# Output projection of a decoder layer: one full-precision product against three products of hi and lo parts

## The chip, the cores and the metric

The kernel runs on one core of one Trainium2 chip. Its time is the device time of one execution in microseconds; the median of the runs is compared. One execution was also taken by the hardware profiler, and all rows below come from that one.

## What is computed

Two layers of a decoder trunk for 512 prompt tokens and 32 sample tokens (T = 544 columns), 1,024 features (8 blocks of 128). Each layer runs a half FFN, a mixer with three branches (chunked gating, forgetting attention, mLSTM), and a second half FFN. The change lies at the end of the mixer:

```python
def merge_branches(ys, gates, w_branch, w_out):
    m = gates[:, :, 0] * (ys[0] @ w_branch[0])
    for nb in range(1, N_BRANCH):
        m = m + gates[:, :, nb] * (ys[nb] @ w_branch[nb])
    return m @ w_out

x = x + mod[:, 1, 2][:, None] * merge_branches((ya, yb, yc), gates, w_branch, w_out)
x = half_ffn(x, mod[:, 2], g_norm[2], w_ff_up[1], w_ff_down[1])
```

## The kernel before

Features lie on the partitions, tokens along the columns; a matmul works on half of the tokens (272 columns). All engines run programs written out by hand, and semaphores order them.

**Two ways to multiply.** Most products (both FFNs, the input projections, the gates) are made of parts. ScalarE copies a block of weights, 128x1024, into a tile of type fp32r ("hi"), and VectorE subtracts that from the raw block, in place, which gives the rest ("lo"). The activations are split in the same way (`HH` and `HX` for the mixer's input). TensorE then adds three fp32r products per pair of blocks: hi by hi, lo of the activations by hi, hi of the activations by lo (`thirds`, L934). The three branch products and the output projection multiply raw fp32 by raw fp32 instead, one `mm` for each pair of blocks; the trace shows such an `mm` as two matmul records.

**Who splits the mixer's weights.** `JOBS` lists the splits in order; `hi_part` (ScalarE, L1416) and `lo_part` (VectorE, L1754) must be called in that order, and `piece` (L437) says where a block's raw weights, hi and lo lie. TensorE waits in `split_in` for the lo.

**The merge.** For each branch (order a, c, b) and each of 8 feature blocks m there are four steps of TensorE: two gate halves (24 fp32r products each) and two branch halves (4 fp32 products each), each half in its own PSUM bank. ScalarE reads a gate half through Tanh (L1451) and then makes the hi of the next block's gate weights. VectorE reads a branch half: (gate + 1) times product (L2066), added to the merged sum `MT` (L2070). With branch b, the last one, the addition raises `s_m`; after its two halves, block m of `MT` is final. This last branch is `LAST_MERGE`.

**The output projection.** TensorE waits for all 16 halves:

```python
pe.wait_ge(s_m, 2 * KD * (l + 1))
apart(pe)
for i in range(OUT_STEPS):
    s = weights(l, f"out{i}")
    w = W[s][:, :].rearrange("p (k n) -> p k n", k=KD)
    for b in range(4):
        product(unit(), [w[:, k, b * P:(b + 1) * P] for k in range(KD)], lambda k: MT[:, k, :])
```

That is 8 output blocks ("units"), each 8 input blocks by 2 halves, 128 `mm` in a layer. Two pairs of PSUM banks take turns, so unit i+2 waits until unit i is read. VectorE reads a unit with the gate into `X` (`add_block`, L1840, called by `add_to_x`), ScalarE squares that block of `X` for the next norm (`squares`, L1344), and the next FFN begins when all 8 squares are summed.

**Weights.** SyncE's queue loads weight steps of 2 MB into two slots in turn, each when the step before in that slot is released. `out0` takes the slot of the last but one merge step, `out1` that of the last; ahead of `out1` the same queue brings `X` back, whose place the lo activations `HX` had held until the last gate.

Of the kernel before, what the change touches and what calls it, by code (L numbers as in the profile page):

```python
# [19 lines left out]
ACT = mybir.ActivationFunctionType  # L20
ALU = mybir.AluOpType
AX = mybir.AxisListType

P = 128
L = 2
D = 1024
KD = D // P
# [3 lines left out]
T = NP + NS  # L31
HALF = T // 2
# [148 lines left out]
JOBS += [(name, i) for name in ("qkc", "vc", "oc") for i in range(4)]  # L181
JOBS += [("qk", i) for i in range(8)] + [("vb", i) for i in range(4)]
JOBS += [("merge", i) for i in range(3 * KD)]
JOB = {job: i for i, job in enumerate(JOBS)}
LAST_GATE = max(u for u, (what, _, _) in enumerate(FILLS) if what.startswith("gate"))

# [87 lines left out]
def build(nc, d, out):  # L274
    ctx = ExitStack()
    with ctx:
# [9 lines left out]
        def sem(name):  # L286
            return ctx.enter_context(nc.semaphore(name))
# [39 lines left out]
        def over(name, start, *shape, dt=F32R):  # L327
            return sb(name, [P] + list(shape), dt, over=area_at + 4 * start)
# [12 lines left out]
        def take(*shape, start=None):  # L341
# [7 lines left out]
            if len(shape) > 1:  # L349
# [67 lines left out]
                        vc=[over(f"w_hi_vc{i}", o_g + 4096 + 1024 * i, 1024) for i in range(4)],  # L417
                        vb=[over(f"w_hi_vb{i}", o, 1024) for i, o in enumerate((o_k + 1280, o_g, o_g + 1024))]
                        + [WHM[0]])
        WFH = over("wfi_hi", o_r - T, KD, 44)  # L420

        G = ctx.enter_context(nc.psum_tensor("g", [P, 4, 512], F32))
# [14 lines left out]
        def piece(l, job):  # L437

            kind, i = job
            if kind == "rows":  # L440
                return None, WFI[:, :, :], WFH[:, :, :], WFL[:, :, :]
            if kind == "qk":
                name, o, hi = ("qb", "kb")[i // 4], None, WHM[i % 2]
            elif kind == "merge":
                name, o, hi = f"{'acb'[i // KD]}{i % KD // 2}", i % 2 * UP_BLOCK, WHM[(i + 1) % 2]
            else:
                name, o = kind, None
                hi = VALUE_HI[kind][i] if kind in VALUE_HI else (LATER_HI if kind == "oc" else FIRST_HI)[i]
            hi = hi[:, :]
            s = slot_of(l, name)  # L450
            if o is not None or kind in VALUE_HI:
                o = i * 1024 if o is None else o
                return name, W[s][:, o:o + 1024], hi, WR[s][:, o:o + 1024]
            cols = slice(i % 4 * P, (i % 4 + 1) * P)
            return (name, W[s][:, :].rearrange("p (k n) -> p k n", k=KD)[:, :, cols],
                    hi.rearrange("p (k n) -> p k n", k=KD), WR[s][:, :].rearrange("p (k n) -> p k n", k=KD)[:, :, cols])
# [91 lines left out]
        s_fd = sem("half_unit_read_by_dve")  # L548
        s_xs = sem("x_stored")
        s_xr = [sem("x_loaded0"), sem("x_loaded1")]  # L550
        s_mh = sem("mixer_weights_hi")
        s_ml = sem("mixer_weights_split")
        s_ks = sem("sample_fox_keys_done")
# [29 lines left out]
        def apart(eng):  # L583

            eng.sem_inc(s_apart, 1)
# [192 lines left out]
        def _(pe):  # L778
# [22 lines left out]
            def unit():  # L801

                p = un.k % 2
                pe.wait_ge(s_dr[p], un.d[p].value())
                un.take()
                return p
# [3 lines left out]
            def weights(l, i):  # L810

                at = AT["mix", (l, i)]
                if asked[0] != at:
                    pe.wait_ge(s_w[at % 2], LANDED[at])
                    asked[0] = at
                return at % 2
# [26 lines left out]
            def product(p, blocks, rhs, m=P, first=None):  # L843

                n = len(blocks)
                for k in range(n):
                    if first is not None:
                        wait(first)
                    for h in range(2):
                        last = mm(G[0:m, 2 * p + h, 0:HALF], blocks[k], rhs(k)[:, h * HALF:(h + 1) * HALF],  # L850
                                  k == 0, k == n - 1)
                last.then_inc(s_unit, 1)
# [78 lines left out]
                while turned:  # L931
                    features(turned.pop())

            def thirds(o, hi, lo, k, h, begin, end):  # L934

                cols = slice(h * HALF, (h + 1) * HALF)
                for i, (w, x) in enumerate(((hi, HH), (hi, HX), (lo, HH))):
                    last = mm(o, w, x[:, k, cols], begin and i == 0, end and i == 2)
                return last

# [71 lines left out]
            for l in range(L):  # L1012
# [279 lines left out]
                turn_back(1)  # L1292
                pe.wait_ge(s_ybs, 2 * (l + 1))
                fill(l, LAST_MERGE, 1)
                pe.wait_ge(s_m, 2 * KD * (l + 1))
                apart(pe)
                for i in range(OUT_STEPS):
                    s = weights(l, f"out{i}")
                    w = W[s][:, :].rearrange("p (k n) -> p k n", k=KD)
                    for b in range(4):  # L1300
                        product(unit(), [w[:, k, b * P:(b + 1) * P] for k in range(KD)], lambda k: MT[:, k, :])
                norm_sums(ada_before(l, 1))
                norm_roots(3 * l + 2, ada_before(l, 1))
                ffn(l, 1)
# [3 lines left out]
        def _(ac):  # L1308
# [32 lines left out]
                outs.n += 1  # L1341
                ac.dma_start(dst, src).then_inc(s_outa, 16)

            def squares():  # L1344
                for k in range(KD):
                    wait(t["xup"])
                    ac.activation(H[:, k, :], X[:, k, :], ACT.Square).then_inc(s_sq, 1)

            def roots(n):

# [10 lines left out]
            def ffn(l, f):  # L1361

                plan, at, ada = ffn_plan(), [0], ada_after(l, f)

                def split():

                    i = at[0]
                    at[0] += 1
                    step, o, n = plan[i]
                    place = AT["ffn", (l, f, step)] % 2  # L1370
                    if i == 0 or plan[i - 1][0] != step:
                        ac.wait_ge(s_w[place], LANDED[AT["ffn", (l, f, step)]])
                    ac.activation(WH[i % 2][:, 0:n], W[place][:, o:o + n], ACT.Copy).then_inc(s_wh, 1)  # L1373

                def after(i):
                    if ada[i] is not None:
                        rows(ADA_ORDER.index(ada[i]))

                def first_splits():
                    ac.wait_ge(s_unit, un.u.value())  # L1380
                    split()
                    split()

                def chunk(c):
                    p = mine()
                    split()
                    drained(ac.activation(halves(SIL[:, c % 2, :]), both(p), ACT.Silu, bias=ZERO[:, 0:1]), p)  # L1387
                    mine()
                    split()

                if l or f:
                    squares()
                first_splits()
                if l or f:
                    roots(3 * l + 2 * f)
                for k in range(KD):
                    wait(t["tn"])
                    ac.activation(HH[:, k, :], TN[:, k % 2, :], ACT.Copy).then_inc(s_hh, 1)
                i = 0
                for blocks in FF_PART:  # L1400
                    for c in range(blocks):
                        chunk(c)
                        if c % 2 == 1:
                            after(i)
                            i += 1
                    for m in range(KD):
                        mine()
                        if at[0] < len(plan):
                            split()
                        if m % 2 == 1:  # L1410
                            after(i)
                            i += 1
# [55 lines left out]
            for l in range(L):  # L1468
# [204 lines left out]
                read(l, IN_SAMPLE.early[-1])  # L1673

                ac.wait_ge(s_outa, outs.value())
                for tick in range(3):
                    read(l, LAST_MERGE.early[tick] + LAST_MERGE.late[tick])
                un.take(KD)
                ffn(l, 1)
            ac.wait_ge(s_outa, outs.value())  # L1680
# [3 lines left out]
        def _(ve):  # L1684
# [69 lines left out]
            def lo_part(l, *jobs):  # L1754

                for job in jobs:
                    assert split[0] == len(JOBS) * l + JOB[job], (job, JOBS[split[0] % len(JOBS)])
                    split[0] += 1
                    _, raw, hi, lo = piece(l, job)
                    ve.wait_ge(s_mh, split[0])  # L1760
                    ve.tensor_tensor(lo, raw, hi, ALU.subtract).then_inc(s_ml, 1)
# [95 lines left out]
                    link(last)  # L1857

            def add_to_x(gate, l):
                for i in range(KD // 2):  # L1860
                    for j in range(2):
                        p = mine()
                        if i % 2 == 0 and j == 0:
                            ve.wait_ge(s_xr[i // 2], 16 * (l + 1))
                        add_block(X[:, bass.ds(i * 2 + j, 1), :].rearrange("p a n -> p (a n)"),
                                  MOD[:, bass.ds(i * 2 + (gate + j), 1), :].rearrange("p a n -> p (a n)"), p, j, True)

            ve.memset(EPSC[:, 0:1], EPS)
            ve.memset(EPSC[:, 1:2], DB * EPS)
# [17 lines left out]
            for l in range(L):  # L1887
# [287 lines left out]
                masked(1)  # L2175
                read(IN_SAMPLE.early[-1])
                own(1)
                for tick in range(3):
                    read(LAST_MERGE.early[tick] + LAST_MERGE.late[tick])
                ve.sem_inc(s_smallf, 1)  # L2180
                add_to_x(24 + 16, l)
                ffn(l, 1)
# [101 lines left out]
```

## Time and profile before

| what | value |
| --- | --- |
| median of 3 runs | 3396.11 us (3390.53 to 3396.54) |
| the profiled execution | 3397.05 us, span 3395.4 us |
| mean granted TensorE clock | 0.958 of 2.4 GHz |
| TensorE busy | 3168.6 us (93%) |
| VectorE busy | 1197.4 us (35%) |
| ScalarE busy | 821.1 us (24%) |
| output projection, each layer | 58.92 us |

Busy time is the union of an engine's instructions; matmuls overlap, so the mean of one (0.29 us) is longer than the time from one to the next. The granted clock is a share of 2.4 GHz.

### The profile page before, as it was taken

The numbers are of one execution on the slowest core, as the hardware profiler recorded it, in microseconds if no ns is written. First come the engines' busy times: TensorE is split into PE (matmuls) and PEld (weight loads), VectorE is DVE, ScalarE is ACT, GpSimd is POOL, SyncE is SP. The second block draws the span as 40 slices with busy tenths as digits, with TensorE's granted clock in tenths as the row PEclk, the third lists the DMA queues.
The fourth block names the chain that finished last, engine by engine and source line by source line (L and its number), as shares of the span: only waits on it lengthen the run. The fifth ranks groups of instructions, "written<-read, shape, count | busy, mean of one in ns | idle before, by whom it ended". The sixth has DMA issues, their size and how long they took to land.

```text
span 3395.4 us, 53600 instructions
## 1 busy us (share of the span) xinstructions
PE 3168.6 (93%) x23198; PEld 2818.9 (83%) x23198; DVE 1197.4 (35%) x2031; ACT 821.1 (24%) x1202; POOL 138.4 (4%) x269
## 2 busy tenths in 40 slices
PE   5999999989799998999989999899888999989999
PEld 4999988758676787999979999787676768889998
DVE  3332334234532214333343333431444322153333
ACT  2211224223431112212222122232234311122121
POOL 0000000000302000000000000000012110000000
PEclk9999999989899999999989999898888999999999
DMA  5444431202138432232313433321021473212221
GB/s 230 149 156 168 149 139 51 88 25 72 60 113 270 149 116 75 100 149 100 112 75 137 161 137 143 132 76 63 27 71 60 159 259 118 108 71 88 93 82 73
DMA packets 117723, 390.76 MB, mean 115 GB/s; under 512 B 12672, under 2 KB 63200, under 8 KB 99184
## 3 DMA queue, kind: packets, MB, share of 16 engines
q1 hardware_dynamic: 99456, 338.36, 27.8%
q0 software_dynamic: 14432, 34.09, 2.9%
q10 hardware_dynamic: 3600, 14.89, 1.1%
q8 instruction: 183, 3.00, 0.4%
q14 instruction: 52, 0.43, 0.0%
HBM read 373.61 MB, written 13.69 MB: 114 GB/s over the span
## 4 chain that ended last, share of the span: by engine, by line
PE 80%; DVE 9%; DMA 5%; ACT 3%; SPq 1%; issue 1%; ACTq 0%; DVEq 0%
PE g L796 72%; PE q L796 4%; PE tb L796 4%; DMA w<-in_w_up 2%; DVE area L2086 1%; DMA area<-in_w_ada 1%; DVE area L1736 1%; DMA area<-in_cache_v 1%; DVE area L1737 1%; DVE w_lo L1795 1%; DVE area L1990 1%; ACT w_hi L1373 1%; DVE h_lo L1748 1%; SPq L660 1%; DMA area<-in_cache_k 0%
## 5 line engine op out<-in xcount | busy, mean ns | idle before, releaser
L796 PE MATMUL g<-h_hi,w_hi 128*128 128x272 f32 x2816 | 593.3, 292 | 37.5 <-DVE h_lo L1748 24.2
L796 PE MATMUL g<-h_hi,w_lo 128*128 128x272 f32 x2816 | 586.8, 290 | 0.0
L796 PE MATMUL g<-h_lo,w_hi 128*128 128x272 f32 x2816 | 583.8, 288 | 0.0
L1373 ACT ACTIVATE w_hi<-w 128x1024 fp32r<-128x1024 f32 (+2 forms) x240 | 274.2, 1144 | 1260.3 <-PE g L796 932.6
L1795 DVE TENSOR_TENSOR w_lo<-w,w_hi 128x1024 fp32r<-128x1024 f32 (+2 forms) x240 | 319.3, 1332 | 509.2 <-ACT w_hi L1373 505.9
L796 PEld LDWEIGHTS g<-h_hi,w_hi 128*128 128x128 f32 x2816 | 446.3, 191 | 59.3 <-ACT area L1387 28.2
L796 PEld LDWEIGHTS g<-h_lo,w_hi 128*128 128x128 f32 x2816 | 445.3, 190 | 0.0
L796 PEld LDWEIGHTS g<-h_hi,w_lo 128*128 128x128 f32 x2816 | 444.4, 190 | 0.0
L796 PE MATMUL g<-h_hi,w_rest 128*128 128x272 f32 x1152 | 341.4, 296 | 0.0
L796 PE MATMUL g<-area,w 128*128 128x272 f32 x1280 | 311.9, 398 | 5.0 <-DVE area L2070 2.6
L796 PEld LDWEIGHTS g<-area,w 128*128 128x128 f32 x1280 | 240.8, 192 | 67.5 <-issue 18.0
L796 PE MATMUL g<-acts_hi,w_hi 128*128 128x272 f32 x1408 | 293.9, 290 | 0.7 <-issue 0.7
L796 PE MATMUL g<-acts_hi,w_lo 128*128 128x272 f32 x1408 | 291.4, 288 | 0.0
L796 PE MATMUL g<-acts_lo,w_hi 128*128 128x272 f32 x1408 | 290.4, 288 | 0.0
L796 PE MATMUL g<-h_hi,w_hi_fill 128*128 128x272 f32 x768 | 243.0, 316 | 33.9 <-DVE area L2066 33.9
L796 PEld LDWEIGHTS g<-acts_hi,w_hi 128*128 128x128 f32 x1408 | 220.9, 188 | 13.3 <-issue 13.3
L796 PE MATMUL g<-h_rest,w_hi_fill 128*128 128x272 f32 x768 | 228.2, 297 | 0.0
L796 PEld LDWEIGHTS g<-h_hi,w_rest 128*128 128x128 f32 x1152 | 227.1, 197 | 0.0
L796 PEld LDWEIGHTS g<-acts_lo,w_hi 128*128 128x128 f32 x1408 | 221.2, 188 | 0.0
L796 PEld LDWEIGHTS g<-acts_hi,w_lo 128*128 128x128 f32 x1408 | 220.0, 189 | 0.0
L796 PEld LDWEIGHTS g<-h_hi,w_hi_fill 128*128 128x128 f32 x768 | 152.2, 198 | 68.9 <-DVE area L2066 38.1
L1842 DVE SCALAR_TENSOR_TENSOR x<-g,mod,x 128x272 f32<-128x272 f32 x80 | 40.1, 501 | 443.9 <-PE g L796 443.9
(268 smaller groups left out, 3813.5 us busy)
## 6 DMA issues: line engine op xcount, KB each, us to landing
w<-in_w_up SPq DMA_DIRECT2D x44, 2048.0 KB, 8.1
w<-in_w_ada SPq DMA_DIRECT2D x32, 2048.0 KB, 8.2
w<-in_w_in SPq DMA_DIRECT2D x16, 2048.0 KB, 8.2
w<-in_w_down SPq DMA_DIRECT2D x16, 1536.0 KB, 7.1
w<-in_w_gate SPq DMA_DIRECT2D x48, 512.0 KB, 5.5
w<-in_w_down SPq DMA_DIRECT2D x16, 1280.0 KB, 5.6
area<-in_cache_k SPq DMA_DIRECT2D x72, 256.0 KB, 4.2
area<-in_cache_v SPq DMA_DIRECT2D x72, 256.0 KB, 4.0
```

What stands on the lines that cost most here:

```text
L660: sp.dma_start(W[slot][:, 2 * UP_BLOCK + q * 512:2 * UP_BLOCK + (q + 1) * 512], d["w_branch"][l * KD + m][:, b * 512:(b + 1) * 512]).then_ ...
L796: return pe.matmul(o, a, b, start=start, stop=stop, skip_group_check=True, **kw)
L1373: ac.activation(WH[i % 2][:, 0:n], W[place][:, o:o + n], ACT.Copy).then_inc(s_wh, 1)
L1736: link(ve.tensor_tensor(halves(o), halves(X[:, k, :]), TB[:, :, 0:HALF], ALU.mult))
L1737: ve.tensor_scalar(o[:, 0:NP], o[:, 0:NP], AMP[:, part, k, 0:1], MOD[:, part * 24 + k, 0:1], ALU.mult, ALU.add)
L1748: ve.tensor_tensor((HX if part == 1 else HL)[:, k - 1, :], TN[:, (k - 1) % 2, :], HH[:, k - 1, :], ALU.subtract)\
L1795: ve.tensor_tensor(WL[i % 2][:, 0:n], W[AT["ffn", (l, f, step)] % 2][:, o:o + n], WH[i % 2][:, 0:n], ALU.subtract).then_inc(s_wl, 1)
L1842: ve.scalar_tensor_tensor(xb[:, 0:HALF], G[:, 2 * p, 0:HALF], gb[:, 0:1], xb[:, 0:HALF], ALU.mult, ALU.add)
L1990: link(ve.reciprocal(d_, d_))
L2086: link(ve.reciprocal(RT[:, m % 2, :], RT[:, m % 2, :]))
```

## The change

The output projection multiplies parts. `MTH` is the hi of the merged sum, made by ScalarE block by block (`merged_hi(m)`), `MTL` its rest, made by VectorE in place of `MT` (`merged_lo(m)`). `merged_hi(m-1)` stands behind the read of the first gate half of block m, `merged_lo(m-1)` behind the second branch half of block m. Eight jobs `("out", i)` split the output weights: 0 and 1 in the merge's last block, 2 and 3 behind it, 4 to 7 during the first four units, on ScalarE behind the square, on VectorE behind `add_block`. In the first unit TensorE waits for each block of `MTL` (`s_mtl`), and in every unit for that unit's weights.

```diff
+JOBS += [("out", i) for i in range(8)]
...
-            def thirds(o, hi, lo, k, h, begin, end):
+            def thirds(o, hi, lo, k, h, begin, end, of=(HH, HX)):
                 cols = slice(h * HALF, (h + 1) * HALF)
-                for i, (w, x) in enumerate(((hi, HH), (hi, HX), (lo, HH))):
+                for i, (w, x) in enumerate(((hi, of[0]), (hi, of[1]), (lo, of[0]))):
                     last = mm(o, w, x[:, k, cols], begin and i == 0, end and i == 2)
...
-                pe.wait_ge(s_m, 2 * KD * (l + 1))
-                apart(pe)
-                for i in range(OUT_STEPS):
-                    s = weights(l, f"out{i}")
-                    w = W[s][:, :].rearrange("p (k n) -> p k n", k=KD)
-                    for b in range(4):
-                        product(unit(), [w[:, k, b * P:(b + 1) * P] for k in range(KD)], lambda k: MT[:, k, :])
+                for i in range(KD):
+                    p = unit()
+                    hi, lo = split_in(l, ("out", i))
+                    for k in range(KD):
+                        if i == 0:
+                            pe.wait_ge(s_mtl, KD * l + k + 1)
+                        for h in range(2):
+                            last = thirds(G[:, 2 * p + h, 0:HALF], hi[:, k, :], lo[:, k, :], k, h, k == 0, k == KD - 1,
+                                          of=(MTH, MTL))
+                    last.then_inc(s_unit, 1)
...
-            def squares():
+            def squares(l=0, then={}):
                 for k in range(KD):
                     wait(t["xup"])
                     ac.activation(H[:, k, :], X[:, k, :], ACT.Square).then_inc(s_sq, 1)
+                    hi_part(l, *then.get(k, ()))
...
-                    squares()
+                    squares(l, {k: [("out", 4 + k)] for k in range(4)} if f else {})
...
-                for tick in range(3):
-                    read(l, LAST_MERGE.early[tick] + LAST_MERGE.late[tick])
+                def merged_hi(m):
+                    ac.wait_ge(s_m, 2 * KD * l + 2 * m + 2)
+                    ac.activation(MTH[:, m, :], MT[:, m, :], ACT.Copy).then_inc(s_mth, 1)
+
+                for u in range(FILL_B, FILL_L):
+                    what, m, h = FILLS[u]
+                    read(l, [u])
+                    if what.startswith("gate") and h == 0 and m:
+                        merged_hi(m - 1)
+                        if m == KD - 1:
+                            hi_part(l, ("out", 0), ("out", 1))
+                merged_hi(KD - 1)
+                hi_part(l, ("out", 2), ("out", 3))
...
+                        if i < 2:
+                            lo_part(l, ("out", 4 + 2 * i + j))
...
-                for tick in range(3):
-                    read(LAST_MERGE.early[tick] + LAST_MERGE.late[tick])
+                def merged_lo(m):
+                    ve.wait_ge(s_mth, KD * l + m + 1)
+                    ve.tensor_tensor(MTL[:, m, :], MT[:, m, :], MTH[:, m, :], ALU.subtract).then_inc(s_mtl, 1)
+
+                for u in range(FILL_B, FILL_L):
+                    what, m, h = FILLS[u]
+                    read([u])
+                    if what.startswith("branch") and h == 1 and m:
+                        merged_lo(m - 1)
+                        if m == KD - 1:
+                            lo_part(l, ("out", 0), ("out", 1))
+                merged_lo(KD - 1)
+                lo_part(l, ("out", 2), ("out", 3))
                 ve.sem_inc(s_smallf, 1)
```

## Rows read from the trace of the kernel before

**Rows 1.** Page of the profile: span, and the chain's shares by engine.

```profile
span 3395.4 us, 53600 instructions
...
PE 80%; DVE 9%; DMA 5%; ACT 3%; SPq 1%; issue 1%; ACTq 0%; DVEq 0%
```

**Rows 2.** Chain in order of time, layer 0's output projection: start, us, what.

```profile
1149.47 71.83 PE g L796 x464
...
1221.38 0.45 DVE area L2066
...
1221.86 0.45 DVE area L2070
1222.31 0.29 issue
1222.60 58.92 PE g L796 x256
```

**Rows 3.** The same chain over the span: long runs of products.

```profile
444.79 52.73 PE g L796 x420
...
1385.35 66.10 PE g L796 x528
...
2908.93 58.92 PE g L796 x256
3000.91 386.10 PE g L796 x3072
```

**Rows 4.** Groups of instructions by line: busy us, mean ns of one.

```profile
L1761 DVE TENSOR_TENSOR w_rest<-w,w_hi_fill 128x1024 fp32r<-128x1024 f32 x66 | 80.7, 1223 | 309.7 <-ACT w_hi_fill L1425 304.3 <-PE g L796 5.4
L1425 ACT ACTIVATE w_hi_fill<-w 128x1024 fp32r<-128x1024 f32 x66 | 69.3, 1051 | 0.2
...
L1347 ACT ACTIVATE h<-x 128x544 f32<-128x544 f32 x48 | 28.5, 648 | 169.4 <-DVE x L1853 120.3 <-PE g L796 43.1 <-DMA x<-in_x 6.0
...
L1748 DVE TENSOR_TENSOR h_lo<-area,h_hi 128x544 fp32r<-128x544 f32 x32 | 23.0, 718 | 0.4
...
L1398 ACT ACTIVATE h_hi<-area 128x544 fp32r<-128x544 f32 x32 | 21.1, 659 | 64.3 <-DVE area L1742 64.3
```

**Rows 5.** Windows: us, busy PE, PEld, DVE, ACT, POOL, granted clock, DMA, GB/s.

```profile
1222.60:1230.60 8.00, 8.00 (x35) 6.67 (x36) 0.39 (x1) 0.00 (x0) 4.75 (x9) 1.00 1.03 398
...
2998.50:3000.90 2.40, 0.00 (x0) 0.00 (x0) 1.23 (x1) 2.37 (x4) 0.00 (x0) 1.00 0.00 0
3000.90:3008.90 8.00, 7.99 (x51) 7.99 (x52) 3.12 (x4) 1.06 (x2) 0.00 (x0) 0.79 0.46 160
67.60:70.00 2.40, 0.05 (x1) 0.05 (x1) 1.23 (x2) 2.37 (x4) 0.00 (x0) 1.00 0.00 0
70.00:78.00 8.00, 8.00 (x64) 8.00 (x65) 3.77 (x5) 2.50 (x3) 0.00 (x0) 1.00 0.47 162
...
668.10:692.00 23.90, 23.84 (x75) 16.34 (x75) 2.89 (x10) 7.46 (x19) 0.00 (x0) 0.60 0.14 58
```

**Rows 6.** Timeline of ScalarE in the last merge steps of layer 0.

```profile
1207.94 0.49 ACT L1451 ACTIVATE area<-g,zero 128x272 f32<-128x272 f32 x1 [1.57 <-PE g L796]
...
1217.65 0.49 ACT L1451 ACTIVATE area<-g,zero 128x272 f32<-128x272 f32 x1 [2.54 <-PE g L796]
```

**Rows 7.** Timeline of VectorE: first and last instruction of one `add_block`.

```profile
1274.21 0.50 DVE L1842 SCALAR_TENSOR_TENSOR x<-g,mod,x 128x272 f32<-128x272 f32 x1 [6.02 <-PE g L796]
...
1275.33 0.19 DVE L1853 TENSOR_TENSOR x<-x,area 128x32 f32<-128x32 f32 x1
```

**Rows 8.** Timeline of SyncE's queue around layer 0's output projection.

```profile
1201.91 0.33 SPq L715 DMA_DIRECT2D w<-in_w_out  x1
1217.69 0.80 SPq L708 DMA_DIRECT2D x<-out_y  x2
1221.31 0.33 SPq L715 DMA_DIRECT2D w<-in_w_out  x1
```

**Rows 9.** DMA issues from 1200 to 1300 us: KB each, us to landing.

```profile
w<-in_w_out SPq DMA_DIRECT2D x2, 2048.0 KB, 9.4
```

More of the change, by code:

```diff
@@ L419, in build @@
                         + [WHM[0]])
+        OUT_HI = [over(f"w_hi_out{i}", o, 1024) for i, o in
+                  enumerate([o_s + 1024 * i for i in range(4)] + [o_p, o_p + 1024, o_g, o_g + 1024])]
+        MTH = over("merged_hi", o_tv, KD, T)
+        MTL = over("merged_lo", o_m, KD, T)
         WFH = over("wfi_hi", o_r - T, KD, 44)
@@ L443, in piece @@
                 name, o, hi = ("qb", "kb")[i // 4], None, WHM[i % 2]
+            elif kind == "out":
+                name, o, hi = f"out{i // 4}", None, OUT_HI[i]
             elif kind == "merge":
@@ L550, in build @@
         s_xr = [sem("x_loaded0"), sem("x_loaded1")]
+        s_mth = sem("merged_hi_done")
+        s_mtl = sem("merged_lo_done")
         s_mh = sem("mixer_weights_hi")
```

## The prediction

> **What bounds the kernel now.** I read the page first: of a span of 3395.4 us, 80% of the chain that ended last is TensorE [rows 1]. So the question is what TensorE does in the output projection, and what it waits for there. The chain in order of time shows both. Layer 0's merge ends at 1149.47 + 71.83 = 1221.3 us; VectorE reads the last branch half (0.45), adds it (0.45), and 0.29 us later TensorE starts: a pause of 1.3 us [rows 2]. Then it runs 58.92 us without a break, in layer 1 the same [rows 2, 3]. That is 128 `mm` (256 records), 0.460 us each. While it runs, ScalarE and VectorE have little to do: an `add_block` lasts from 1274.21 to 1275.52, 1.31 us, behind 6.02 us of idleness [rows 7], and a square 0.65 us [rows 4]. So the stage is bound by TensorE alone, and the run of `mm`, the pause ahead of it and the clock are all that can move.
>
> **The products.** 128 `mm` become 384 fp32r products of the same 272 columns. Their pace stands in three runs: 52.73 us for 420 (0.1256 each), 66.10 for 528 (0.1252), 386.10 for 3072 (0.1257, with a slow beginning in it, see the clock) [rows 3]. The first of these is a projection whose hi and lo lie as those of `out` will: hi in a tile of its own, lo as a strided part of the 2 MB slot. I take 0.1252: 384 x 0.1252 = 48.1 us for 58.92, a gain of 10.8 us in a layer. Between 0.1252 and 0.1257 it is 10.8 to 10.7.
>
> The Trainium skill ("TensorE: Matmul & The Clock Gate", section "Back-to-back issue gap") gives the time from one warm matmul to the next as columns / 2.4 GHz + 2.5 ns. For 272 columns that makes an estimate of 0.1158 us, where the runs show 0.1252. By it the gain would be 58.92 - 44.5 = 14.4 us in a layer.
>
> **The pause ahead of it.** Today VectorE's last addition releases TensorE. After the change the first unit needs the lo of `out` 0, and on VectorE two instructions come between. First `merged_lo(6)`, a subtraction over 128x544: 0.72 us as its like at L1748 [rows 4]; it waits for nothing, because ScalarE makes the hi of block 6 during the gates of block 7. Then `lo_part("out", 0)`, over 128x1024: 1.22 us [rows 4]. With some 0.04 us from one to the next that is 2.0 us: TensorE starts at 1222.60 + 2.0 = 1224.6, and the pause grows from 1.3 to 3.3 us. That is +2.0 us in a layer. Its lower bound is 1.22 + 0.65 (pipelined) = 1.9; upper, if every hop cost the 0.29 us that TensorE's release costs, 2.5.
>
> What follows on VectorE doesn't hold TensorE. `out` 1 is split by 1225.6 and the last block of `MTL` by 1226.4; ScalarE's hi of that block needs 0.66 us from 1222.3 on [rows 4]. The first unit wants block 7 after 42 products, 5.3 us after its start, at 1229.9, so 3.5 us are to spare, and unit 1 wants its weights at 1230.6. The waits for blocks 0 to 6 are met before they are asked; I cost them at nothing, since the runs of rows 3 hold a wait at each unit too.
>
> **The clock.** This is the term that a count of instructions leaves out. After the pause of 1.3 us the granted clock of the next 8 us is 1.00, the level of 2.4 GHz [rows 5]. After the pause of 2.4 us at 2998.5, with TensorE busy at 2.4 GHz before it, the next 8 us have a mean of 0.79: part of them at 1.2 GHz, and 51 products begin where 64 do at 1.00 [rows 5]. Of the four pauses of this length ahead of an FFN's main part, three look so and one, at 67.6, does not [rows 5]. A pause of 3.3 us is longer than these, so I take the fall as the rule: 8 x 0.21 = 1.7 us lost in each layer. Bounds: nothing (as at 70.0) and, twice that, 3.4.
>
> **Work moved into the merge.** Per block m, ScalarE gets one copy of 128x544 (0.66 us) and VectorE one subtraction (0.72 us). ScalarE's slot is the gap between its reads of the two gate halves: at block 6 it is idle for 1.57 us there, after its 1.05 us copy of the next weights [rows 6, 4]. So 0.9 us remain. At block 7 there are no next gate weights and 2.54 us of idleness [rows 6]; the new work is 0.66 + 2 x 1.05 = 2.76 us, so the second Tanh comes 0.2 us late. Late next would be the second branch half, which reuses that bank; but TensorE first runs the other branch half, 4 `mm` x 0.46 = 1.8 us, and the Tanh needs 0.49 [rows 2, 6]. Cost nothing; without that cover 0.2 us. VectorE's four instructions and one split leave most of a block's 9.7 us free (from one second Tanh to the next, 1207.94 to 1217.65 [rows 6]). If every block's 0.66 us did reach TensorE, it would be 8 x 0.66 = 5.3 us in a layer.
>
> **The splits of `out` 4 to 7.** In the first four units VectorE does `add_block` (1.31), then waits for ScalarE's square and copy (0.65 + 1.05), then subtracts (1.22): 4.3 us with hops, in a unit of 48 x 0.1252 = 6.0 us [rows 3, 4, 7]. Bank pairs come free after `add_block`, ahead of all that, and `out` 4 is split more than 12 us before unit 4 begins, so no step waits. The copy for `out` 4 also needs the second 2 MB. They are issued at 1221.31 when the last merge step is done, and the order on the queue, with `X` ahead of them, does not change; with 9.4 us they land at 1230.7 [rows 8, 9]. ScalarE asks at 1224.6 + 6.0 + 1.31 + 0.65 = 1232.6 or later, so 1.9 us are to spare; a late landing would hold VectorE, then the reading of unit 1, and TensorE only at unit 3, 12 us on. `out` 0, issued at 1201.91, lands by 1211.3, and is asked for at 1217.65 - 2.54 = 1215.1 at the earliest [rows 6, 8, 9]. The stage after the last unit is untouched: nothing is split there any more.
>
> **The sum.** In a layer -10.8 + 2.0 + 1.7 = -7.1 us, in two -14.2. The profiled execution took 3397.05 us, 0.94 above the median of the runs; from the median, 3396.11 - 14.2 = 3382.
>
> **Rivals.**
> 1. The clock stays at 2.4 GHz after the pauses, as at 70.0 [rows 5]. Then -10.8 + 2.0 = -8.8 in a layer, 3396.1 - 17.6 = 3378.5; with the fall in one layer 3380. For it speaks one pause of the four; the length alone does not decide, since pauses of 2.4 us went both ways [rows 5].
> 2. The merge slows, because splits and copies on ScalarE push the Tanh, and with it TensorE's banks: +5.3 in a layer, 3382 + 10.6 = 3392.5, within 0.2% of before. Against it stand the free 0.9 us at each block.
> 3. Slower than before: the clock falls at the pause and does not come back in the stage. At 668.1, after a wait, 23.9 us ran at 0.60 [rows 5]. At that level the 48.1 us become 80, and a layer costs +32 - 10.8 + 2.0 = +23 us: 3442. It decides from 8.8 us lost in a layer on, 17.6 us at 1.2 GHz. Against it: TensorE was fed sparsely there, 75 records in 23.9 us, while here it would run without a break, as from 3000.90 on, where the whole run of 386 us keeps 0.1257 a product [rows 3].
> 4. The products are paced by their columns alone: 272 columns at the granted 2.4 GHz are 0.1133 us, 43.5 us for 384, and with it 4.6 us less in a layer: 3382 - 9.2 = 3373. No run of products in this trace is that fast [rows 3]. The Trainium skill's rule named above comes nearest to this case.
> 5. The change does not do what it says: products of parts fall back to the time of a full `mm`. Then 384 x 0.460 instead of 48.1 us would be +117 in a layer, far out; the pieces have the type that rows 3 show at 0.125, so I give it next to nothing.
>
> **How the numbers follow.** Forecast 3382 with a chance of 0.62; rival 1 0.22; rival 2 0.06; rival 3 0.03; rival 4 0.04; the rest, with rival 5, 0.03. The forecast's own range is 3380 to 3385 (a pause between 1.9 and 2.5 us longer, up to 1.7 us more lost to the clock in one layer). The runs before lie between 3390.5 and 3396.5, so a median can be off by 2 or 3 us. The range reaches over rival 1 and that scatter: 3375 to 3388. Under 0.2%, 6.8 us, a measurement of this kernel can hardly tell from no change. Below 3389.3 lie the forecast and rivals 1 and 4 with part of the rest: faster 0.90, same 0.06 (rival 2), slower 0.04.
>
> **What would show it.** Right: two output projections of about 50 us as one run of 384 products; ahead of each a pause of 3.3 us that ends with VectorE's subtraction at L1761's like; a granted clock near 0.79 in the 8 us after it; blocks of the merge no longer than the 9.7 us of before; the 33 us between the last unit and the FFN's main part unchanged. Wrong: gaps between units (then an owner of a split is late), a pause above 4 us, longer merge blocks, or a clock under 0.9 over the whole stage.

## The result, and the profile after

The kernel after the change takes 3368.85 us (median of 5 runs, 3362.14 to 3378.00) beside 3394.98 us of the kernel before (5 runs, 3383.36 to 3396.54): a ratio of 0.9935, 95% interval 0.9907 to 0.9962. It is faster, as forecast, but by more, and lies below the range of 3375 to 3388. The profiled execution took 3377.30 us.

The page of the kernel after, the span and the chain's shares by engine [rows 1]:

```profile
span 3375.6 us, 54188 instructions
...
PE 83%; DVE 8%; DMA 3%; ACT 3%; SPq 1%; issue 1%; ACTq 0%; DVEq 0%
```

The chain in order of time, from the merge's last long run through the output projection, in layer 0 and in layer 1 (start, us, what) [rows 2, 3]:

```profile
1158.10 71.81 PE g L805 x464
1229.91 3.02 issue
1232.92 49.98 PE g L805 x384
...
1282.93 0.50 DVE x L1866
...
2823.44 71.81 PE g L805 x464
2895.25 3.02 issue
2898.27 49.98 PE g L805 x384
```

The merge's run of 464 is as long as before (71.83). The pause is 3.02 us for 1.3, the products are one run of 384 in 49.98 us for 58.92. From the merge's end to the last product it was 1.3 + 58.92 = 60.2 us, now it is 53.0: 7.2 us less in each layer, 14.5 in both. From there to the FFN's main part it is 33.1 us (1282.9 to 1316.0), as before.

Windows of the kernel after, the first 8 us of the two runs and the rest of each (columns as in [rows 5]):

```profile
1232.90:1240.90 8.00, 7.97 (x51) 8.00 (x52) 4.12 (x5) 0.61 (x1) 4.78 (x9) 0.79 0.99 381
2898.30:2906.30 8.00, 8.00 (x52) 8.00 (x53) 4.12 (x5) 0.56 (x1) 0.00 (x0) 0.79 0.64 274
1240.90:1282.80 41.90, 41.90 (x335) 41.77 (x333) 12.91 (x32) 8.41 (x11) 0.00 (x0) 1.00 0.15 54
2906.30:2948.20 41.90, 41.90 (x339) 41.75 (x338) 12.86 (x32) 8.40 (x11) 0.00 (x0) 1.00 0.14 51
```

TensorE is busy throughout, yet 51 and 52 products begin in the first 8 us, at a granted clock of 0.79, where 64 do at 1.00. In the rest of the stage the clock is 1.00.

VectorE's timeline around the pause in layer 0:

```profile
1230.49 0.44 DVE L2097 TENSOR_TENSOR area<-area 128x272 f32<-128x272 f32 x1
1230.96 0.72 DVE L2207 TENSOR_TENSOR merged_lo<-area,merged_hi 128x544 fp32r<-128x544 f32 x1
1231.61 2.35 DVE L1785 TENSOR_TENSOR w_rest<-w,w_hi_out 128x1024 fp32r<-128x1024 f32 x2
1233.88 0.72 DVE L2207 TENSOR_TENSOR merged_lo<-area,merged_hi 128x544 fp32r<-128x544 f32 x1
1234.51 2.35 DVE L1785 TENSOR_TENSOR w_rest<-w,w_hi_out 128x1024 fp32r<-128x1024 f32 x2
```

Behind the last addition (L2097) come the rest of block 6 and the splits of `out` 0 and 1, merged here into one row of 2.35 us; TensorE starts at 1232.92, when the first of the two, 1.22 us long, is done. ScalarE's second gate halves of the last blocks of the merge:

```profile
1206.88 0.49 ACT L1464 ACTIVATE area<-g,zero 128x272 f32<-128x272 f32 x1 [1.05 <-PE g L805]
...
1216.57 0.49 ACT L1464 ACTIVATE area<-g,zero 128x272 f32<-128x272 f32 x1 [1.03 <-PE g L805]
...
1226.28 0.49 ACT L1464 ACTIVATE area<-g,zero 128x272 f32<-128x272 f32 x1
```

They are 9.69 and 9.71 us apart, 9.7 before [rows 6]. The copies of the merged blocks shrank ScalarE's idleness ahead of them from 1.57 to about 1.0 us, and the copies in the last block used up its 2.54 us; the merge's run on TensorE is no longer for it.

### The profile page after: what moved, and what is told of

Same layout as the page of the kernel before. It is cut to its first block, busy times and chain, and to the rows that moved or that the text cites. A ratio compares the mean times of both kernels' runs of the same rounds, so it can differ in the third digit from the quotient of the medians.

```text
span 3375.6 us, 54188 instructions
## 1 busy us (share of the span) xinstructions
PE 3149.5 (93%) x23454; PEld 2821.6 (84%) x23454; DVE 1228.7 (36%) x2063; ACT 847.1 (25%) x1234; POOL 138.6 (4%) x269
## 4 chain that ended last, share of the span: by engine, by line
PE 83%; DVE 8%; DMA 3%; ACT 3%; SPq 1%; issue 1%; ACTq 0%; DVEq 0%
PE g L805 74%; PE q L805 5%; PE tb L805 4%; DVE area L2113 1%; DMA area<-in_w_ada 1%; DVE area L1760 1%; DMA area<-in_cache_v 1%; DMA w<-in_w_up 1%; DVE area L1761 1%; DVE area L2017 1%; DVE h_lo L1772 1%; SPq L669 1%; DMA area<-in_cache_k 1%; PE tb L808 0%; DVE w_rest L1785 0%
## 5 line engine op out<-in xcount | busy, mean ns | idle before, releaser
L805 PE MATMUL g<-area,w 128*128 128x272 f32 x768 | 194.1, 402 | 2.4 <-ACT w L1464 1.6
L1785 DVE TENSOR_TENSOR w_rest<-w,w_hi_fill 128x1024 fp32r<-128x1024 f32 x66 | 80.8, 1224 | 297.4 <-ACT w_hi_fill L1438 291.9
```

What stands on the lines that cost most here:

```text
L805: return pe.matmul(o, a, b, start=start, stop=stop, skip_group_check=True, **kw)
```

## The experiments

**Theories.** The first is the prediction's: the change acts in the output projection alone, by a shorter run of products, a longer pause and the clock behind it, 14.5 us in all by the profile; the rest of the measured difference is scatter of the runs. Its rivals put the rest, or the gain itself, elsewhere: in the order and the splits, in an effect of each layer outside its stage, or in weight loads that land sooner. The expectations number theories as they came up.

The kernel before ran 106 times in all, the 12 runs of "before again" among them: mean 3390.9 us, median 3391.4, 3377.4 to 3406.4, standard deviation 5.8. In the table the difference is from that mean, with 1.96 standard errors (a 95% interval, somewhat narrow for 5 or 6 runs); the stage is the change of "merge's end to last product" over both layers in that kernel's own profiled execution, one execution for each row but that of after.

| kernel | median us (runs) | ratio [95%] to before beside it | mean less 3390.9 | stage |
| --- | --- | --- | --- | --- |
| before again | 3392.5 (12) | 0.9998 [0.9983, 1.0012] | +0.7 ±3.8 | 0 |
| after, all 17 runs | 3373.4 (17) | (below) | -18.4 ±2.6 | -14.5 |
| early splits | 3365.1 (6) | 0.9918 [0.9900, 0.9937] | -27.5 ±3.5 | -23.1 |
| full products, new order | 3393.95 (12) | 1.0012 [0.9998, 1.0027] | +4.9 ±2.7 | +6.8 |
| layer 0 alone | 3385.8 (12) | 0.9983 [0.9971, 0.9994] | -5.6 ±2.4 | -7.2 |
| layer 1 alone | 3382.5 (12) | 0.9983 [0.9965, 1.0001] | -5.9 ±4.1 | -8.7 |
| longer pause | 3377.1 (9) | 0.9959 [0.9944, 0.9974] | -14.5 ±2.6 | -8.3 |
| before, GpSimd padded | 3389.9 (12) | 0.9999 [0.9983, 1.0015] | -0.8 ±3.5 | 0 |
| before, TensorE padded at its head | 3443.7 (5) | 1.0163 [1.0140, 1.0186] | +52.3 ±2.9 | 0 |
| after, TensorE padded at its head | 3428.6 (6) | 1.0112 [1.0091, 1.0134] | +35.8 ±3.7 | -14.5 |
| before, hidden padding, 512 | 3391.5 (12) | 1.0010 [0.9997, 1.0024] | +2.3 ±3.8 | 0 |
| before, hidden padding, 256 | 3389.8 (12) | 1.0003 [0.9989, 1.0017] | +0.1 ±3.0 | 0 |

**Both kernels again.** No edit: the kernel before against itself, and the kernel after two more times.

> The kernel before, unchanged, timed against itself. Theory 1 (what the change gains is in the output projection alone, 7.2 us in a layer, and the rest of the measured difference is scatter between executions): the medians differ by up to 10 us without any change, the interval of the ratio holds 1.000, and in the profile the stretch from the end of the merge to the end of the last unit is 60.2 us in both layers while the mixers differ by several us from those of the first profile. Theory 2 (the change also speeds up other stages, for good): executions of the kernel before agree within 0.1%, 3 us, and its stages repeat.

> The changed kernel again. Theory 1: 14.5 us under before within the scatter, ratio near 0.9957; merge end to last unit 53.0 us or less in each layer (51.3 where the clock does not fall after the pause); the mixers of layer 0 and layer 1 are no longer +8 and -13 us against the first profile of before, but fall anywhere in some 15 us. Theory 2: 20 to 26 us under before, ratio 0.9925 to 0.9940, and layer 1's mixer again 13 us shorter.

> The changed kernel a third time, beside the two one-layer kernels on the same chip. Theory 1: the median within 3372 to 3382, ratio near 0.996. Theory 3: again 18 to 24 us under before, ratio 0.993 to 0.995. In both, the stage itself repeats: a pause of 3.0 us and 50.0 us of products, or 48.4 where the clock does not fall.

Before against itself gave 0.9998 [0.9983, 1.0012]. After gave 3372.46 us (0.9940 [0.9923, 0.9958]) and 3374.64 us (0.9947 [0.9928, 0.9966]); its 17 runs have a mean of 3372.5. So the median of the first five runs of after is low by 3.6 us, and the median of before from which the prediction started, 3396.11, is high by 5.2. The stage is 3.02 us and 49.97 to 49.99 us in both layers of all three profiles. The totals don't decide between theories 1 and 2: theory 1's ratio of 0.9957 and theory 2's 0.9940 both lie in both intervals. The shorter mixer of layer 1 that theory 2 asks for did not come back: from VectorE's last update of `X` in the first half FFN to its first in the projection it is 727.7 us in the first profile of after, 735.0 and 737.8 in the other two.

**Early splits: the pause taken away.** The rests of `out` 0 and 1 are made between the last gate half and the last branch halves, so that none stands between the last addition and the first unit:

```diff
                     p = unit()
+                    if i == 0 and p == 1:
+                        pe.wait_ge(s_fd, 48 * (l + 1))
                     hi, lo = split_in(l, ("out", i))
...
+                    if what.startswith("gate") and h == 1 and m == KD - 1:
+                        lo_part(l, ("out", 0), ("out", 1))
                     if what.startswith("branch") and h == 1 and m:
                         merged_lo(m - 1)
-                        if m == KD - 1:
-                            lo_part(l, ("out", 0), ("out", 1))
```

> The changed kernel with the splits of out 0 and out 1 on VectorE moved ahead of the last two branch halves, so that the first unit finds its weights ready; TensorE waits, where the first unit takes the branch's banks (layer 0), for the last branch half to be read. If the pause of 3.0 us and the clock that falls after it cost what the profile says (3.0 + 1.7 us in a layer): pause about 0.9 us in layer 0 and about 0.1 in layer 1, granted clock 1.00 in the next 8 us, merge end to last unit about 49.2 and 48.4 us, 8 us less in all than the changed kernel, ratio to before near 0.993. Rival: the wait only moves, because VectorE reads the last branch halves late; then the merge grows by 1 to 3 us in its last block, and the gain over the changed kernel is under 4 us.

The chain in order of time of this kernel, both layers, and its windows in the first 8 us of the products:

```profile
1143.23 71.81 PE g L805 x464
1215.04 0.65 issue
1215.69 48.47 PE g L805 x384
...
2810.56 120.04 PE g L805 x848
```

```profile
1215.70:1223.70 8.00, 8.00 (x64) 8.00 (x65) 5.31 (x9) 2.92 (x4) 4.24 (x8) 1.00 1.00 415
2882.40:2890.40 8.00, 8.00 (x66) 8.00 (x66) 5.83 (x10) 3.17 (x4) 0.00 (x0) 1.00 1.02 433
```

In layer 0 the pause is 0.65 us, in layer 1 merge and products are one run (120.04 - 71.81 = 48.2 us for the products). The clock stays at 1.00, and 384 products take 48.47 us. Pause and clock are gone together: 49.1 and 48.2 us where after has 53.0, 8.7 us less over both layers; the means differ by 3372.5 - 3363.4 = 9.1 ±4.1. This is the fastest kernel of the study.

**The new order with the old products.** All of the change stays (order, waits, splits), but the projection multiplies raw `MT` by raw `w_out`, 128 full products. So that both stay raw, the rests are written over their own hi:

```diff
-        MTL = over("merged_lo", o_m, KD, T)
+        MTL = MTH
...
-                            last = thirds(G[:, 2 * p + h, 0:HALF], hi[:, k, :], lo[:, k, :], k, h, k == 0, k == KD - 1,
-                                          of=(MTH, MTL))
+                            last = mm(G[:, 2 * p + h, 0:HALF], w[:, k, :], MT[:, k, h * HALF:(h + 1) * HALF],
+                                      k == 0, k == KD - 1)
```

> The changed kernel's order of work, all its splits and all its waits, but the output projection multiplies raw weights by the raw merged sum, 128 full-precision products as before; the lo parts are computed into the hi tiles and not used. It prices the added work and the pause alone. Theory 1: merge end to last unit 3.0 + 58.9 + about 1.7 us of lower clock = 63.6 us against 60.2, so 3.4 us more in a layer, 6.8 us slower than before in all, within scatter of ratio 1.002. Theory 2 (the order of work itself speeds up other stages): as fast as before or faster by some us, although its own stage is longer.

```profile
1148.41 71.82 PE g L808 x464
1220.24 3.02 issue
1223.25 60.61 PE g L808 x256
```

This chain holds the two costs by themselves: 3.02 us for 1.3, and 60.61 us for 58.92. The same 256 records take 1.69 us more behind the longer pause. By the stage it should be 6.8 us slower than before; it is 4.9 ±2.7 slower, as theory 1 has it. The merge work and the splits cost nothing in it (71.82), so the gain of the change comes from the products alone.

**One layer at a time.** A constant `NEW` chooses the layer that gets the change, the other keeps the code of before:

```diff
+                if l == NEW:
                     for i in range(KD):
                         p = unit()
...
+                else:
+                    pe.wait_ge(s_m, 2 * KD * (l + 1))
...
```

> The change in layer 0 only; layer 1 keeps the full-precision product. So far the changed kernel is some 20 us faster than before, of which 14.5 lie between the end of the merge and the last unit. Theory 1 (each layer gains 7.2 us in its own stage, the remaining 6 us are scatter): -7.2 us, ratio near 0.998; layer 1's stage 60.2 us again. Theory 3 (layer 1's other stages run better because they begin at another time against the transfers and the clock): -10 to -13 us, ratio near 0.9965, and layer 1 gains 3 us or more outside its output projection in this profile too.

> The change in layer 1 only. Theory 1: -7.2 us, ratio near 0.998, and the sum of this run's gain and that of the layer-0 kernel is 14.5 us. Theory 3: nothing ahead of layer 1's merge moves, so -7 us here and 10 to 13 in the layer-0 kernel.

The chain of the kernel with layer 1 alone:

```profile
1148.48 71.84 PE g L812 x464
...
2906.77 3.02 issue
2909.78 48.47 PE g L812 x384
```

The window of its first 8 us of products (columns as in [rows 5]):

```profile
2909.78:2917.78 8.00, 8.00 (x64) 8.00 (x65) 5.11 (x8) 0.93 (x2) 0.00 (x0) 1.00 0.66 281
```

Each layer gives about its stage, 5.6 ±2.4 and 5.9 ±4.1 us, and no more. So there is no extra gain that each layer brings outside its stage: that rival falls. And a pause of 3.02 us doesn't always cost the clock: here the 384 products ran in 48.47 us, at a granted clock of 1.00 from the first 8 us on. Over all profiles such pauses ahead of the projection stand 12 times, 11 with the fall and one without. Where the other runs of this kernel had the fall, its stage is -7.2 and not -8.7.

**A longer pause.** The first unit also waits for the rest of `out` 2:

```diff
-                    hi, lo = split_in(l, ("out", i))
+                    hi, lo = split_in(l, ("out", i if i else 2))
+                    hi, lo = piece(l, ("out", i))[2:]
...
-                            lo_part(l, ("out", 0), ("out", 1))
+                            lo_part(l, ("out", 0), ("out", 1), ("out", 2))
...
-                lo_part(l, ("out", 2), ("out", 3))
+                lo_part(l, ("out", 3))
```

> The changed kernel with the first unit held until out 2 is split as well, two subtractions of 1.22 us later: the pause doubled nearly, from 3.0 to 5.4 us. If the pause is paid in full and the clock falls once after it, as it does after 3.0 us: +2.4 us in a layer, 4.8 us slower than the changed kernel, products still 50.0 us. Rival: the longer pause brings a longer stretch at 1.2 GHz, products 51 to 52 us, and 7 to 9 us slower. Rival: the pause is hidden by something later in the layer, then no slower than the changed kernel.

```profile
1146.55 71.82 PE g L805 x464
1218.37 5.29 issue
1223.66 50.79 PE g L805 x384
```

The pause grows by 2.27 us, as expected. The products take 50.79 us here and 50.73 in layer 1, not the 50.0 expected: the loss behind the pause grows to 50.79 - 48.47 = 2.3 us, and the granted clock of the next 8 us is 0.67 and 0.68 where it was 0.79. So the rival of a longer stretch at 1.2 GHz is the nearer one. By the stage it is 6.1 us slower than after, by the means 3.9 ±3.3 (3376.4 for 3372.5), which doesn't tell the expected 4.8 from 6.1.

**Is the rest in the weight loads?** In the profiles of after the 2 MB loads land sooner than in before, from the first FFN on, ahead of any changed instruction, and the page counts two more packets of instructions. To separate this from the change, 512 semaphore increments were put into an engine's program (`for _ in range(512): apart(pe)`): at TensorE's head in before and in after, at the end of GpSimd's in before.

> The kernel before, with 512 semaphore increments that nobody waits for at the head of TensorE's program, where TensorE waits 20.9 us for its first operands anyway. So far every build with the whole change lands its 2 MB weight loads in 7.7 to 7.9 us, and every other build in 8.1 to 8.4, from the first FFN on, ahead of the first changed instruction; the whole change also makes TensorE's program some 512 instructions longer (185 packets of instructions for 183). Theory 4 (the 5 us that the changed kernel gains outside its stage come with the program as it is loaded, not with what the change does): 185 packets, loads in 7.7 to 7.9 us, the first FFN's waits for split weights fall from some 3 to under 1 us, and about 4 to 5 us faster than before, ratio near 0.9985. Rival (the loads follow from something else in the change): 8.1 to 8.4 us and the time of before, ratio 1.000.

> The kernel before, with the same 512 increments at the end of GpSimd's program, behind its last page load, where it has nothing left to do. If the length of any program counts: loads in 7.7 to 7.9 us and 4 to 5 us faster. If only TensorE's program counts: as before, 8.1 to 8.4 us, ratio 1.000.

> The changed kernel with the 512 increments at the head of TensorE's program. Theory 4: the landing time of its 2 MB loads changes once more or stays, but it is what the time outside the stage follows: at 7.7 us the time of the changed kernel, 3372; at 8.1 to 8.4 us some 5 us slower, 3377, which is before less the 14.5 us of the stage. The stage itself repeats: a pause of 3.0 us and 50.0 us of products.

At TensorE's head they cost time of their own: the first matmul begins at 79.79 us for 20.90, and the first FFN's main part at 120.81 for 69.95. With its loads at 7.8 us the kernel before is then 52.3 ±2.9 us slower for a delay of 50.9, which leaves +1.4 ±2.9: this speaks against a gain of 4 to 5 us from the loads. It rests on the delay read in one execution each; in the profiles of before and before again alone this main part begins at 69.95 and 71.66. The kernel after, its loads slowed to 8.1 us, is 54.2 ±4.3 us slower than without the increments for a delay of 50.8 to 52.6 (120.75 us for 68.19 to 69.97 in its three profiles), which decides nothing. Then the increments were placed where TensorE waits anyway:

```diff
+                for _ in range(34):
+                    apart(pe)
                 pe.wait_ge(s_rsx, n + 1)
...
                 last.then_inc(s_rs, 1)
+                for _ in range(28):
+                    apart(pe)
...
+            for _ in range(100):
+                apart(pe)
             pe.wait_ge(s_cst, 16)
...
                 ffn(l, 1)
-
+            for _ in range(40):
+                apart(pe)
```

> The kernel before with 512 more instructions in TensorE's program (semaphore increments, nothing computed differs), this time placed where TensorE waits anyway: 100 at its head, 34 ahead of each of the six waits for the inverse roots, 28 behind each, 40 at its end. Theory: a longer TensorE program makes the 2 MB loads land sooner, and that alone is the 4 to 5 us that the changed kernel gains outside the output projection. Then the loads land in 7.7 to 7.8 us as with 512 at the head (185 instruction packets) and the ratio is near 0.9987, 4 to 5 us faster than the kernel before. Rival: the loads land sooner but TensorE's waits in the FFNs are hidden on the whole, and the gain has another source: 1.000, within 1.5 us. A cost of the increments that shows in spite of their places would make it slower than 1.000; the time from the last product of an FFN to the next main part says so (33 us before).

> The kernel before with 256 more instructions in TensorE's program at the same places (50, 17, 14, 20). It has as many more as the kernel with the change in one layer only, whose loads landed in 8.1 to 8.4 us. If the length of TensorE's program alone sets the landing, 184 instruction packets and loads of 8.1 to 8.4 us, ratio 1.000. If any padding quickens the loads, 7.7 us and some 0.9987 as with 512.

The DMA view over the whole span (queue: packets, MB, share; and the loads of `w_up`, KB each, us to landing): before, before with 512 and with 256 hidden increments, after, and after with 512 at its head:

```profile
q8 instruction: 183, 3.00, 0.4%
...
w<-in_w_up SPq DMA_DIRECT2D x44, 2048.0 KB, 8.1
```

```profile
q8 instruction: 185, 3.03, 0.4%
...
w<-in_w_up SPq DMA_DIRECT2D x44, 2048.0 KB, 7.8
```

```profile
q8 instruction: 184, 3.01, 0.4%
...
w<-in_w_up SPq DMA_DIRECT2D x44, 2048.0 KB, 8.3
```

```profile
q8 instruction: 185, 3.03, 0.4%
...
w<-in_w_up SPq DMA_DIRECT2D x44, 2048.0 KB, 7.7
```

```profile
q8 instruction: 187, 3.06, 0.4%
...
w<-in_w_up SPq DMA_DIRECT2D x44, 2048.0 KB, 8.1
```

That TensorE's program moves the landing is shown: the same 512 increments take the kernel before from 8.1 to 7.8 us and the kernel after from 7.7 to 8.1, and half of them, or 512 for GpSimd (8.2), do nothing of the kind.

What that is worth, the hidden increments don't settle, because at one of their places they were not hidden. The first FFN's main part in the chain of before (x288), and the chain up to it in before with 512 hidden increments (main part x192):

```profile
69.95 36.27 PE g L796 x288
```

```profile
40.69 3.53 PE tb L796 x16
44.52 5.30 issue
49.81 2.17 PE tb L796 x4
...
75.38 25.82 PE g L796 x192
```

The 34 increments ahead of the first roots' products take 5.30 us in which nothing else holds TensorE, and the main part begins 5.4 us later. At the norms behind it nothing is lost (from the sums to the roots' products 9.13 us for 9.21 at the first of them). So of the +2.3 ±3.8 us of this kernel 5.4 are the increments' own, and -3.2 ±3.8 are left: a gain of 4 to 5 us from the loads fits this as well as none. With half the increments the main part begins at 70.08, and loads and total stay as they were.

The traces say a little more. Take the half FFNs from VectorE's first update of `X` on, that is without the mixers and the output projections. They take 1595.5 to 1596.9 us in the profiles of before, before again and before with GpSimd padded, and 1592.2 to 1592.8 in the three of after, so most of what after gains outside its stage shows there. With quick loads the kernel before takes 1594.9 (head) and 1595.5 (hidden), and the kernel after with slow ones 1594.3. By these single executions the loads give a part of it at most.

## Why the prediction was right, and where it was wrong

**The products.** Predicted 48.1 us at full clock, 0.1252 each; measured 48.47 (early splits, layer 1 alone), 0.1262 each, and 48.2 where the products follow the merge without a pause. From one start to the next it is 0.1256 in the second half of the run in every profile that has the new products. The run was taken up to 0.4 us too short in a layer, and the gain of 10.45 lies below the stated 10.7 to 10.8. Rival 4 (0.1133 each) falls. The estimate worked out from the Trainium skill ("TensorE: Matmul & The Clock Gate", section "Back-to-back issue gap"), 0.1158 us, isn't reached in any run here; the section gives that formula for an isolated matmul and says that the spacing in a stream of weight loads and matmuls is another. Here each product has its own weight load (64 and 65 in the first 8 us at 1.00), and the rows of the kernel before were the better guide.

**The pause.** Predicted 3.3 us, measured 3.02, so 1.7 us longer than before where the stated bounds were 1.9 and 2.5. The two instructions between the last addition and the first unit are the named ones. In the timeline the split begins 0.07 us before the subtraction ahead of it ends, where the prediction put 0.04 us between them, and TensorE starts 0.1 us behind the split, where it kept the 0.29 us of before.

**The clock.** Predicted a granted clock of 0.79 in the next 8 us and 1.7 us lost; measured 0.79 and 1.5 (49.98 for 48.47), with the old products 1.69. Both layers showed it in every profile of after, so rival 1 falls for these executions, though one pause of 12, in layer 1 alone, went its way. Rival 3 falls too: the rest of the stage ran at 1.00.

**The merge and the splits.** Predicted nothing, measured 71.81 us for 71.83 and no gap in the 384 products. Rival 2 falls, and the full products in the new order show it by the total. Rival 5 falls with the pace of the products.

**The sum.** -7.1 us in a layer predicted, -7.2 measured, and the early splits show pause and clock as its costs by removing both. That the two numbers are so close is partly luck: the products gave 0.35 us less than forecast, pause and clock cost 0.3 and 0.2 less, and these errors cancel.

**What failed is the step "How the numbers follow", and with it the base of the sum.** The sum started from the median of three runs, put everything outside the output projection at nothing, and the step said that a median can be off by 2 or 3 us, because the three runs lay within 6 us of each other. The measured 3368.85 lies 6 us under the range, and the mean of all 17 runs, 3372.5, still 2.5 under it. The runs of one kernel have a standard deviation of 5.8 us. A median of three is then off by about 1.25 x 5.8 / 1.73 = 4.2 us, one of five by about 3.2, and their difference by 5.3, one standard deviation. The distance from 3382 to 3368.85, 13.1 us, comes apart like this:

- 5.2: the median from which the sum started, 3396.11, lies above the mean of 106 runs, 3390.9.
- 3.6: the five runs of after lie below the mean of its 17 (3368.85 for 3372.5).
- 0.3: the stage, -14.5 for -14.2.
- 3.9 ±2.6: a gain outside the output projection (-18.4 for -14.5), which the prediction had at nothing.

Of these the first two are scatter, and with a base of 3390.9 the same terms would have given 3376.7, inside the range. The last one stays open, and it is what the terms lacked. Early splits and the longer pause show it too (-4.4 ±3.5, -6.2 ±2.6 beyond their stages), the full products in the new order hardly (-1.9 ±2.7), and one layer alone doesn't (+1.6 ±2.4, +2.8 ±4.1). All these differences share the same mean of before, so they are not independent. A share that each layer brings by itself is excluded. Quicker loads through a longer TensorE program are not: the increments at the head and the half FFNs in the traces speak against them as the whole cause, the hidden increments leave them open. The profiles place most of the gain in the half FFNs; what makes it, or whether chance has a part in a difference of 0.1%, no run here shows.

## What to carry to other kernels

Cost a faster run of products together with the pause ahead of it: here the work that stands between the last addition and the first product, and the stretch at 1.2 GHz behind it, ate 1.7 + 1.5 of 58.92 - 48.47 = 10.45 us in each layer, and making the first splits one step earlier gave all of it back. Take a term for a stage from rows of the stage, and the width of the range from the scatter of many runs: three runs that lie close together say little about where a median will fall. A gain that is left over after the stage is accounted for should be tested by itself, since a plausible companion of it (here the loads) need not be its cause. Where such a test adds instructions, read from the trace at every place what they cost: here one place of many took 5.4 us, more than the effect looked for.

## What the runs showed of the hardware that was not expected

- The median landing of the 2 MB loads of `w_up`, issued by another engine, went with the length of TensorE's program: 7.7 to 7.8 us with 185 packets of instructions, 8.1 to 8.4 with 183, 184 and 187, whatever the added instructions were. That the total time follows it is not shown.
- Pauses of the same 3.02 us were followed by a stretch at 1.2 GHz in 11 of 12 cases; two of 5.29 us cost 2.3 us instead of 1.5, one of 0.65 us nothing.
- The time of a run goes with its mean granted clock, which lay between 0.954 and 0.964 in the 101 runs of before that have it on record: over these, 2.5 us less for each 0.001 more, and beside this line a standard deviation of 3.2 us remains of 5.8.
- A semaphore increment on TensorE took about 0.156 us: 34 of them held it for 5.30 us ahead of the first roots' products, and 512 at its head put the first matmul at 79.79 us, an estimate that takes them to start with the span. With 100 at its head, 15.6 us by this, the first matmul began at 21.06 us for 20.90.
